# Three places instead of four for each of two rings of gathers, two more page buffers, and four compression items asked for early

## The chip, the cores and the metric

One NeuronCore of a Trainium2 chip runs the whole program. The metric is the time of one execution on the device, in us; shown is the median of three.

## The reference, cut to what matters

One layer of a decoder for 256 prompt tokens and 8 x 4 sample tokens, all in float32: an input projection; stick-breaking attention (part A) and native sparse attention (part B: compressed, selected and window keys) over a paged cache; an output projection; a layer norm; and a feed-forward part that picks single neurons out of a table of 16384.

```python
def nsa_cmp_slc(...):            # part B, sample tokens: 8 sequences, 16 cached pages each
    kcmp = compress(rows[0], ...)  # windows of 32 rows, stride 16, through w1, gelu, w2
    vcmp = compress(rows[1], ...)
    ...                            # scores on kcmp choose 16 blocks of 64; attend to them and to the window
def peer_ffn(x, w_query, sub_keys, u_tab, v_tab):
    q = (xc @ w_query).reshape(PEER_TBLOCK, PEER_HEADS, 2, PEER_QDIM // 2)
    s = jnp.einsum('thcd,ckd->thck', q, sub_keys)
    ...                            # top 16 x 16 per head, best 16 of their sums: experts, gate
    act = jax.nn.gelu(jnp.einsum('thkd,td->thk', u_tab[experts], xc))
    return jnp.einsum('thk,thkd->td', gate * act, v_tab[experts])
```

Per token 8 heads x 16 experts: 128 rows of 8 KB out of `peer_u` and as many out of `peer_v`.

## The kernel before, in words

Every engine has an instruction stream of its own, written out by hand; semaphores alone order them. What the change touches:

**Slots.** The 288 tokens are 9 groups of 32, and each group has 32 slots of 4 experts. A slot is one gather of 128 rows of 8 KB (1 MB) from `peer_u`, a dot of it with the tokens on DVE (`gather_dot`, L2716), and later one gather from `peer_v`, which PE multiplies with a diagonal of weights (`value_rows`, L1955). All engines go through the slots as "ticks" s = 0 to 287. POOL (L2865) issues at tick s first u(s), then v(s - 11) (LAG = 11). u(s) waits until dot s - 4 is done, v(s) until PE has used v(s - 4): four places each, `u_ring` = ring[4:8], `v_ring` = ring[0:4] (L623). POOL runs in order, so whatever waits holds the rest. The weights of a round of 8 slots are made after its last dot (`act_start`, `act_finish`). The last 8 value gathers (TAIL, L242) alternate between both rings, since the dots no longer need theirs.

**The ring before that.** The same 8 places of 1 MB hold w_in, the pages of part A, w_out (L714) and then the 16 blocks of w_query, loaded by SP (`load`, L691; the place of block k is WQ_AT, L277). Place 8 (`AT_T + 4096`) is a ninth, for blocks 7 and 12. PE multiplies the blocks in order (`query_rows`, L1618), which yields the scores that DVE picks experts from. v(0) to v(3) wait until the last query block of their place is used.

**Pages.** The cached rows of part B come as items of 8 pages of 128 KB (1 MB), each page with its own DMA and a page number that the issuing engine first reads into a register (L462). `Background` (L302) gives each of them one of four buffers of 1 MB, `later_rows` (L604). 32 compression items (16 for keys, 16 for values) use buffers 2 and 3 alone, since buffers 0 and 1 hold w1. After them come, per half of the batch, 8 items ks, 2 kw, 8 vs, 2 vw, then 16 blocks of w_out and 16 of w_query for the last tokens, all through four buffers. A buffer is asked for again when PE has used what was in it (`later_used`). SP asks for the even pages and ACT, at ticks fixed in the program (`odd_pages` L1029, `odd_rows` L1038, ODD_PAGES L215), for the odd ones; of the first two compression items SP asks for all 8. PE handles compression item n at ticks from 10 + 5n // 2 (`taps`, L1678), the attention of the halves from ticks 92 and 111, ahead of the value matmuls of the same tick.

**SP's order around the gathers' start** (L714 to L746): w_out, w1, w_query 7, 0 to 6, 8 to 15; then it waits for `saved` (DVE has moved what the buffers overwrite, L2344), for h_in 5 (second tile normalized, L2382) and until block 12 is used; then compression item 0 and on.

Of the kernel before, what the change touches and what calls it, by code (L numbers as in the profile page):

```python
# [145 lines left out]
RING = 8  # L146
# [4 lines left out]
SWAP_AT = {STEP[ms[-1]] + 2: n for n, ms in enumerate(ROPED)}  # L151
ROUND = 8
# [47 lines left out]

def odd_page_ticks():
# [40 lines left out]
TAIL = SLOTS_ALL - 8  # L242


def tail_buffer(s):

    return "uv"[s % 2 == 0], (s - TAIL) // 2 % 4, (s - TAIL) // 8

# [28 lines left out]
WQ_AT = (4, 5, 6, 0, 1, 2, 3, 8, 0, 1, 2, 3, 8, 0, 1, 2)  # L277


WQ_LAST = [max(k for k in range(16) if WQ_AT[k] == s) for s in range(4)]  # L280


class Stream(Items):


    def __init__(self):
        super().__init__(RING + 1)
# [14 lines left out]
class Background(Items):  # L302


    def __init__(self):
        super().__init__(4)
        for i in range(4 * NB):
            self.add(("cmp", i // 16, i % 16), 2 + i % 2, 8)
        self.last[0] = self.last[1] = self.n - 1
        k = 0  # L310
        for h in range(2):
            for name, count, dmas in (("ks", 8, 8), ("kw", 2, 1), ("vs", 8, 8), ("vw", 2, 1)):
                for i in range(count):
# [57 lines left out]
def hybrid_step(nc, dram, outs):  # L371
    stream, later_items = Stream(), Background()
    with ExitStack() as ctx:
# [45 lines left out]
        ring = [words(AT_RING + 2048 * s, 2048) for s in range(RING)] + [words(AT_T + 4096, 2048)]  # L419
# [26 lines left out]
        ring_full = [sem(f"ring_full{s}") for s in range(RING + 1)]  # L446
# [157 lines left out]
        later_rows = [words(AT_T + 2048 * k, 2048) for k in range(4)]  # L604
# [18 lines left out]
        u_ring, v_ring = ring[4:8], ring[0:4]  # L623
# [5 lines left out]
        u_full = [sem(f"u_full{k}") for k in range(4)]  # L629
        v_full = [sem(f"v_full{k}") for k in range(4)]  # L630
# [3 lines left out]
        later_full = [sem(f"later_full{k}") for k in range(4)]  # L634
# [43 lines left out]
        def _(sp):  # L678
# [57 lines left out]

            sp.wait_ge(saved, 1)
# [41 lines left out]
        def _(act):  # L779
# [412 lines left out]
        def _(pe):  # L1192
# [762 lines left out]
            def value_rows(s):  # L1955
# [36 lines left out]
        def _(dve):  # L1992
# [723 lines left out]
            def gather_dot(s):  # L2716
# [3 lines left out]
                dve.wait_ge(u_full[j % 4], 16 * (s // 4 + 1))  # L2720
                u = u_ring[j % 4].rearrange("p (a b) -> p a b", a=KT)
# [78 lines left out]
        def _(pool):  # L2800
# [130 lines left out]
```

## Time and profile before

| what | us |
|---|---|
| median of three timed runs | 2435.42 (2432.51 to 2435.45) |
| the profiled execution, its own time | 2443.28 |
| its span | 2441.4 |
| PE busy | 1761.5 (72%) |
| DVE busy | 1301.4 (53%) |
| POOL busy | 863.1 (35%) |
| DMA: 961.30 MB, mean over the span | 394 GB/s |
| gathers, POOL's queue: 626.31 MB | 62.3% of 16 engines' time |
| SP's and ACT's transfers: 300.39 and 32.65 MB by queue | 31.8% and 4.0% |

The span counts from the first to the last record on the core. The page (a printed summary of the profile) says "the share of 16 engines' span" for a DMA queue: the time its packets took, over 16 engines and the span; overlapping packets can bring a share over 1. PE is the matrix engine, DVE the vector engine, ACT the scalar engine, POOL and SP the two that mostly issue DMAs here; a "q" behind a name is its queue of issued DMAs. L and a number is the line.

### The profile page before, as it was taken

The page shows a single profiled execution, that of the slowest core. Times are in us where ns is not written, and L with a number is a line of the kernel's source. Part 1 is how long each engine was busy: PE and PEld are TensorE (multiplying, and loading weights), DVE is VectorE, ACT ScalarE, POOL GpSimd, SP SyncE. Part 2 cuts the span into 40 slices and gives each one's busy share as a digit, 9 for nine tenths or more (in the row PEclk, how much of TensorE's full clock was granted, in tenths as well). Part 3 has the DMA queues.
Part 4 walks back from the last instruction along what each step waited for, and adds up shares of the span by engine and source line. Part 5 has one row for each costly group of instructions (what it writes and reads, how often), then busy time and mean ns, then how long its engine had stood idle before and what let it go on. Part 6 is the DMA issues. An engine that isn't in the chain of part 4 may idle for free.

```text
span 2441.4 us, 30395 instructions
## 1 busy us (share of the span) xinstructions
PE 1761.5 (72%) x9939; PEld 977.9 (40%) x9939; DVE 1301.4 (53%) x2580; ACT 356.9 (15%) x837; POOL 863.1 (35%) x595
## 2 busy tenths in 40 slices
PE   8999999989998987778675656869633333346334
PEld 6777766643786765556412212217300000000000
DVE  0600112352876886666959562345788754555553
ACT  0001111330411111210201020012210001012111
POOL 0000000000133433444424242324465677677673
PEclk9999999999998988888887877978755555555556
DMA  9989999998699999999999999999999999999997
GB/s 386 374 344 360 371 384 371 368 374 363 274 396 407 384 407 409 406 407 406 409 385 399 386 365 398 420 421 421 419 421 421 421 422 421 421 421 422 421 421 320
DMA packets 213311, 961.30 MB, mean 394 GB/s; under 512 B 23841, under 2 KB 89378, under 8 KB 122754
## 3 DMA queue, kind: packets, MB, share of 16 engines
q0 software_dynamic: 84432, 626.31, 62.3%
q1 hardware_dynamic: 92914, 300.39, 31.8%
q10 hardware_dynamic: 35808, 32.65, 4.0%
q8 instruction: 80, 1.31, 0.2%
q14 instruction: 77, 0.63, 0.1%
HBM read 952.77 MB, written 14.88 MB: 396 GB/s over the span
## 4 chain that ended last, share of the span: by engine, by line
DMA 43%; PE 41%; issue 5%; DVE 4%; ACTq 4%; POOL 1%; SPq 1%; ACT 1%; POOLq 0%; DVEq 0%
DMA sb<-in_peer_v,sb 24%; PE bank L1208 14%; DMA sb<-in_nsa_t 12%; PE bank L1688 6%; PE bank L1971 4%; DMA sb<-in_peer_u,sb 3%; PE bank L1574 3%; PE bank L1279 2%; PE bank L1621 2%; ACTq L462 2%; PE bank L1307 2%; DMA sb<-in_nsa_v 2%; DVE sb L2722 2%; DMA sb<-in_w_out 1%; PE bank L1886 1%
## 5 line engine op out<-in xcount | busy, mean ns | idle before, releaser
L2722 DVE CUSTOM_DVE_ANT_0 sb<-sb 128x2048 f32<-128x2048 f32 x288 | 659.4, 2292 | 411.0 <-DMA sb<-in_peer_u,sb 403.3
L1971 PE MATMUL bank<-sb 128*32 128x512 f32 x2304 | 461.2, 852 | 473.1 <-DMA sb<-in_peer_v,sb 447.2
L2838 POOL DMA_INDIRECT sb<-in_peer_v,sb x288 | 505.5, 1755 | 561.8 <-PE bank L1971 504.0
L2838 POOL DMA_INDIRECT sb<-in_peer_u,sb x288 | 349.3, 1213 | 433.5 <-DVE sb L2722 241.7
L1971 PEld LDWEIGHTS bank<-sb 128*32 128x32 f32 x2304 | 60.6, 126 | 773.8 <-DMA sb<-in_peer_v,sb 700.8
L1208 PE MATMUL bank<-sb 128*128 128x288 f32 x1408 | 352.1, 410 | 7.5 <-DMA sb<-in_tokens_t 7.5
L1688 PE MATMUL bank<-sb 128*128 128x256 f32 x1024 | 281.7, 435 | 86.6 <-DMA sb<-in_nsa_t 70.6
L1208 PEld LDWEIGHTS bank<-sb 128*128 128x128 f32 x1408 | 266.5, 191 | 92.1 <-issue 13.9
L1688 PEld LDWEIGHTS bank<-sb 128*128 128x128 f32 x1024 | 250.2, 310 | 130.7 <-DMA sb<-in_nsa_t 85.1
L1165 ACT ACTIVATE sb<-sb 128x32 f32<-128x32 f32 x288 | 86.2, 315 | 669.3 <-PE bank L1971 306.3
L2822 POOL DMA_DIRECT2D out_a<-sb x1 | 0.5, 545 | 503.9 <-PE bank L1307 503.9
L1754 PE MATMUL bank<-sb 128*32 128x512 f32 x128 | 71.7, 753 | 41.2 <-DMA sb<-in_nsa_t 41.2
L1808 PE MATMUL bank<-sb 128*32 128x256 f32 x256 | 62.0, 423 | 35.1 <-DMA sb<-in_nsa_v 35.1
L786 ACT ACTIVATE sb<-bank 128x288 f32<-128x288 f32 x44 | 18.1, 410 | 410.1 <-PE bank L1208 410.1
L969 ACT ACTIVATE sb<-sb 32x2048 f32<-32x2048 f32 x36 | 68.6, 1907 | 51.8 <-PE bank L1777 29.5
L1574 PE MATMUL bank<-sb 128*32 128x512 f32 (+1 forms) x256 | 71.8, 600 | 0.1
L1621 PE MATMUL bank<-sb 128*128 128x160 f32 (+1 forms) x512 | 71.0, 297 | 0.7 <-issue 0.7
L1621 PEld LDWEIGHTS bank<-sb 128*128 128x128 f32 x512 | 67.7, 191 | 3.3 <-ACT sb L982 2.2
L1307 PE MATMUL bank<-sb 128*32 128x512 f32 x512 | 61.5, 602 | 5.6 <-DMA sb<-in_a_v 5.5
L1886 PE MATMUL bank<-sb 128*128 128x128 f32 x512 | 62.5, 284 | 3.5 <-DMA sb<-in_w_query 3.5
L1886 PEld LDWEIGHTS bank<-sb 128*128 128x128 f32 x512 | 60.2, 198 | 11.7 <-DMA sb<-in_w_query 7.6
L1847 PE MATMUL bank<-sb 128*32 128x512 f32 x512 | 60.7, 622 | 2.0 <-DMA sb<-in_w_out 1.9
(412 smaller groups left out, 1486.9 us busy)
## 6 DMA issues: line engine op xcount, KB each, us to landing
sb<-in_a_k SPq DMA_DIRECT2D x128, 512.0 KB, 7.3
sb<-in_a_v SPq DMA_DIRECT2D x128, 512.0 KB, 7.1
sb<-in_w_in SPq DMA_DIRECT2D x43, 1024.0 KB, 9.4
sb<-in_w_out SPq DMA_DIRECT2D x32, 1024.0 KB, 20.9
sb<-in_w_query SPq DMA_DIRECT2D x32, 1024.0 KB, 10.0
sb<-in_nsa_t SPq DMA_DIRECT2D x200, 128.0 KB
sb<-in_nsa_t ACTq DMA_DIRECT2D x184, 128.0 KB
sb<-in_nsa_v SPq DMA_DIRECT2D x64, 128.0 KB
```

The costliest lines, as they stand in the source:

```text
L969: act.activation(replica(g)[32 * q:32 * q + 32], src, ACT.Copy).then_inc(rep_in, 1)
L1165: act.activation(diag[j % 4], const["fold"], ACT.Copy, scale=w8[:, r % 2, j:j + 1]).then_inc(diag_in, 1)
L1208: mm = pe.matmul(bank[step % 2][:, 0:T], w[:, kt * P:(kt + 1) * P], x_t[:, kt, :], start=(kt == 0), stop=(kt == KT - 1))
L1307: mm = pe.matmul(bank[(0 if half else 6) + c][r, :], z_t[:, half, 2 * pp + j, r], rows[b4][:, 1024 * j + 512 * c:1024 * j + 512 * c + 512] ...
L1574: mm = pe.matmul(bank[3 * (n % 2) + tt][own, :], mix(4 * kq + kt)[:, P * tt:P * tt + rows], w[:, kt, :], start=(kq == 0 and kt < parts), s ...
L1621: mm = pe.matmul(bank[5 if m == 1 else 1 if m == 2 else m % 2][:, 0:count], w[:, P * kt:P * kt + P], h_t[:, kt, 0:count], start=(kt == 0), ...
L1688: mm = pe.matmul(bank[(7, 3)[n % 2]][:, 0:256], rows[:, :, l], w1_one[:, :, l, :], start=(l == 0), stop=(l == 15), skip_group_check=True)
L1754: mm = pe.matmul(bank[((5, 6), (7, 2))[ph][c]][32 * b4:32 * b4 + 32, :], q_pad[:, 4 * h + b4, g], rows[:, 4 * c:4 * c + 4, g, :], start=(g ...
L1886: mm = pe.matmul(bank[2 + m % 2][:, 0:ROWS_2], w[:, P * kt:P * kt + P], h_t2[:, kt, :], start=(kt == 0), stop=(kt == KT - 1))
L1971: mm = pe.matmul(bank[g % 2][32 * c:32 * c + 32, :], diag[j % 4], rows[:, 512 * c:512 * c + 512], start=(s in FIRST), stop=(s in LAST), sk ...
L2722: dve.tensor_tensor_reduce(out=u, in0=u, in1=replica(g), scale=1.0, scalar=0.0, op0=ALU.mult, op1=ALU.add, accum_out=act8[:, r % 2, j:j + ...
L2838: pool.indirect_dma_start(rows[j % 4], None, dram[table], bass.IndirectOffsetOnAxis(ap=idx, axis=0)).then_inc(full[j % 4], 16)
```

## The change: what it does

- `PLACES = 3`: u_ring is ring[4:7], v_ring ring[0:3]; u(s) waits for dot s - 3, v(s) for PE's use of v(s - 3).
- v(0), v(1), v(2) are issued at ticks 9, 10, 11 instead of 11, 12, 13; v(3) and on at tick s + 11 as before.
- TAIL is the last 6 slots, alternating between the rings, each place once.
- `later_rows` gets ring[7] and ring[3]: the compression items go through buffers 2 to 5, the rest through six. ACT asks for the odd pages of item n + 4, not n + 2, when item n is used, and for the first six ks items at ticks 82, 84, 87, 89, 90, 91 instead of 89 to 92 for the first four.
- The ninth place for query blocks is gone. Blocks 0 to 7 go to places 4, 5, 6, 7, 1, 2, 0, 3, blocks 8 to 15 to 1, 2, 0 in turn.
- SP asks for all 8 pages of compression items 0 to 3 itself, and earlier: item 0 after `saved`, ahead of the query blocks; item 1 after h_in 5; item 2 when block 3 is used (its place 7 is buffer 4); item 3 when block 7 is used (place 3, buffer 5). Item 4 and on come behind block 15, even pages by SP.

```diff
+PLACES = 3
...
+FIRST_ODD = (82, 84, 87, 89, 90, 91)
...
-            at = order[k - 4][3] + 1 if k >= 4 else NSA_AT[0] - 3 + k
+            at = order[k - 6][3] + 1 if k >= 6 else FIRST_ODD[k]
...
-TAIL = SLOTS_ALL - 8
+TAIL = SLOTS_ALL - 2 * PLACES
...
-    return "uv"[s % 2 == 0], (s - TAIL) // 2 % 4, (s - TAIL) // 8
+    return "uv"[s % 2 == 0], (s - TAIL) // 2
...
-WQ_AT = (4, 5, 6, 0, 1, 2, 3, 8, 0, 1, 2, 3, 8, 0, 1, 2)
+WQ_AT = (4, 5, 6, 7, 1, 2, 0, 3, 1, 2, 0, 1, 2, 0, 1, 2)
...
-        super().__init__(4)
+        super().__init__(6)
         for i in range(4 * NB):
-            self.add(("cmp", i // 16, i % 16), 2 + i % 2, 8)
+            self.add(("cmp", i // 16, i % 16), 2 + i % 4, 8)
         self.last[0] = self.last[1] = self.n - 1
-        k = 0
+        k = 2
...
-                    self.add((name, h, i), k % 4, dmas)
+                    self.add((name, h, i), k % 6, dmas)
...
-        later_rows = [words(AT_T + 2048 * k, 2048) for k in range(4)]
+        later_rows = [words(AT_T + 2048 * k, 2048) for k in range(4)] + [ring[7], ring[3]]
...
-        u_ring, v_ring = ring[4:8], ring[0:4]
+        u_ring, v_ring = ring[4:4 + PLACES], ring[0:PLACES]
...
-            for k in (7, *range(7), *range(8, 16)):
-                load(("wq", k), dram["w_query"][k].rearrange("p k n -> p (k n)"))
...
             sp.wait_ge(saved, 1)
+            cached_rows(0, 0, range(8))
+            query_blocks(range(8))
             sp.wait_ge(h_in, 5)
-            sp.wait_ge(item_used, stream.used["wq", 12])
+            cached_rows(0, 1, range(8))
+            sp.wait_ge(item_used, stream.used["wq", 3])
+            cached_rows(0, 2, range(8))
+            query_blocks(range(8, 11))
+            sp.wait_ge(item_used, stream.used["wq", 7])
+            cached_rows(0, 3, range(8))
+            query_blocks(range(11, 16))
             for kv in range(2):
                 for i in range(2 * NB):
-                    later_pages(("cmp", kv, i), 8 * i, lambda pg: dram["nsa_t"][bass.ds(pg, 1), kv],
-                                range(8) if kv == 0 and i < 2 else range(0, 8, 2))
+                    if kv or i >= 4:
+                        cached_rows(kv, i, range(0, 8, 2))
...
-                    if 2 * NB * kv + i + 2 < 4 * NB:
-                        odd_pages(2 * NB * kv + i + 2)
+                    if 2 * NB * kv + i + 4 < 4 * NB:
+                        odd_pages(2 * NB * kv + i + 4)
...
-                if s >= 4:
-                    hold(u_used, s - 3)
+                if s >= PLACES:
+                    hold(u_used, s - PLACES + 1)
...
-                    ring_of, k, turn = tail_buffer(s)
-                    if turn:
-                        hold(v_used, s - 7)
-                    elif ring_of == "v":
-                        hold(v_used, TAIL - 3 + k)
+                    ring_of, k = tail_buffer(s)
+                    if ring_of == "v":
+                        hold(v_used, TAIL - PLACES + 1 + k)
                     else:
-                        hold(u_used, SLOTS_ALL - 3 + k)
+                        hold(u_used, SLOTS_ALL - PLACES + 1 + k)
...
-                if s >= LAG:
+                if LAG - 2 <= s < LAG + PLACES - 2:
+                    v_of(s - LAG + 2)
+                elif s >= LAG + PLACES:
                     v_of(s - LAG)
```

`query_blocks(ks)` loads the named blocks of w_query as the removed loop did, and `cached_rows(kv, i, pages)` is the removed call of `later_pages`. Elsewhere the change only writes `s % PLACES` and `s // PLACES` for the place of a slot and its count.

## Rows read from the trace of the kernel before

**Rows 1.** The page, parts 4 and 5: the chain, and the dots

```profile
DMA 43%; PE 41%; issue 5%; DVE 4%; ACTq 4%; POOL 1%; SPq 1%; ACT 1%; POOLq 0%; DVEq 0%
...
L2722 DVE CUSTOM_DVE_ANT_0 sb<-sb 128x2048 f32<-128x2048 f32 x288 | 659.4, 2292 | 411.0 <-DMA sb<-in_peer_u,sb 403.3
```

**Rows 2.** Windows: us, each engine's busy us, PE clock, DMA share, GB/s

```profile
602.00:618.00 16.00, 16.00 (x53) 6.58 (x55) 2.39 (x7) 0.69 (x1) 0.00 (x0) 1.00 0.04 15
636.00:648.00 12.00, 11.52 (x172) 10.97 (x171) 10.56 (x44) 7.13 (x11) 0.17 (x1) 1.00 0.02 8
648.00:699.00 51.00, 51.00 (x361) 47.76 (x361) 47.95 (x130) 19.34 (x38) 11.40 (x12) 1.00 1.00 410
699.00:702.00 3.00, 3.00 (x23) 2.68 (x22) 2.73 (x9) 0.85 (x3) 1.88 (x2) 1.00 0.63 175
790.00:839.00 49.00, 43.43 (x221) 32.78 (x220) 41.90 (x95) 7.04 (x30) 12.87 (x14) 0.89 1.02 399
839.00:842.00 3.00, 3.00 (x15) 3.00 (x14) 2.79 (x9) 0.00 (x0) 2.60 (x2) 1.00 0.48 123
1240.00:1280.00 40.00, 29.97 (x127) 8.40 (x130) 13.74 (x30) 1.24 (x4) 9.89 (x8) 0.91 1.03 379
1433.00:1438.00 5.00, 5.00 (x53) 1.98 (x55) 1.57 (x3) 0.00 (x0) 0.09 (x1) 0.78 0.31 94
1524.00:2402.00 878.00, 455.11 (x2481) 128.34 (x2479) 514.73 (x905) 120.64 (x276) 520.71 (x318) 0.60 1.01 421
2402.00:2406.00 4.00, 1.93 (x8) 0.20 (x8) 2.94 (x9) 0.44 (x3) 2.54 (x1) 0.50 0.62 219
```

**Rows 3.** Timeline of SP's queue: start, us to the last one's end, count

```profile
589.34 0.43 SPq L693 DMA_DIRECT2D sb<-in_w_query  x1
...
617.15 6.33 SPq L693 DMA_DIRECT2D sb<-in_w_query  x7
...
647.52 36.97 SPq L693 DMA_DIRECT2D sb<-in_w_query  x8
...
699.01 13.70 SPq L731 DMA_DIRECT2D sb<-in_nsa_t  x16
```

**Rows 4.** Waits of SP, 560 to 1000: total us, times, longest

```profile
SPq L739 <- PE bank L1621: 9.9, 1, 9.9
```

**Rows 5.** Timeline of DVE: what fires `saved` and h_in 5

```profile
563.72 0.68 DVE L2344 COPY sb<-bank 32x512 f32<-32x512 f32 x1
...
632.72 2.34 DVE L2382 SCALAR_TENSOR_TENSOR sb<-sb 32x2048 f32<-32x2048 f32 x1
```

**Rows 6.** Timeline of PE: query block 11, item 0's taps, first value matmul

```profile
684.63 4.61 PE L1621 MATMUL bank<-sb 128*128 128x160 f32 x32
...
714.15 9.05 PE L1688 MATMUL bank<-sb 128*128 128x256 f32 x32 [3.20 <-issue]
...
723.13 1.07 PE L1971 MATMUL bank<-sb 128*32 128x512 f32 x8
```

**Rows 7.** Timeline of POOL: gathers, in brackets its idle time before

```profile
687.42 0.94 POOL L2838 DMA_INDIRECT sb<-in_peer_u,sb  x1 [3.12 <-DVE sb L2722]
...
699.72 0.94 POOL L2838 DMA_INDIRECT sb<-in_peer_v,sb  x1 [6.18 <-PE bank L1621]
...
725.04 2.46 POOL L2838 DMA_INDIRECT sb<-in_peer_v,sb  x1 [6.72 <-PE bank L1971]
...
1814.54 3.06 POOL L2838 DMA_INDIRECT sb<-in_peer_u,sb  x1 [5.90 <-DVE sb L2722]
...
2406.69 0.94 POOL L2838 DMA_INDIRECT sb<-in_peer_v,sb  x1 [2.15 <-PE bank L1971]
```

**Rows 8.** DMA issues, 640 to 700: count, KB each, median us to landing

```profile
sb<-in_w_query SPq DMA_DIRECT2D x8, 1024.0 KB, 10.0
```

**Rows 9.** The chain: a value gather from issue to landing, steady and last

```profile
1997.53 17.05 DMA sb<-in_peer_v,sb
...
2415.40 15.88 DMA sb<-in_peer_v,sb
```

More of the change, by code:

```diff
@@ L274, in add @@
         self.used[key] = self.n
-WQ_AT = (4, 5, 6, 0, 1, 2, 3, 8, 0, 1, 2, 3, 8, 0, 1, 2)
-WQ_LAST = [max(k for k in range(16) if WQ_AT[k] == s) for s in range(4)]
+WQ_AT = (4, 5, 6, 7, 1, 2, 0, 3, 1, 2, 0, 1, 2, 0, 1, 2)
+WQ_LAST = [max(k for k in range(16) if WQ_AT[k] == s) for s in range(PLACES)]
 class Stream(Items):
     def __init__(self):
-        super().__init__(RING + 1)
+        super().__init__(RING)
         order = []
@@ L318, in __init__ @@
             for i in range(16):
-                self.add((name, i), k % 4, 1)
+                self.add((name, i), k % 6, 1)
                 k += 1
@@ L418, in hybrid_step @@
         x_t = words(AT_X, KT, T)
-        ring = [words(AT_RING + 2048 * s, 2048) for s in range(RING)] + [words(AT_T + 4096, 2048)]
+        ring = [words(AT_RING + 2048 * s, 2048) for s in range(RING)]
         def mix(kt):
@@ L445, in hybrid_step @@
         item_used = sem("item_used")
-        ring_full = [sem(f"ring_full{s}") for s in range(RING + 1)]
+        ring_full = [sem(f"ring_full{s}") for s in range(RING)]
         consts_in, first_in, x_in, wg_in, rope_in, w1_in, pages_in = (sem(n) for n in (
@@ L628, in hybrid_step @@
         q_in, s_mm, s_in, gate_arg, gate_e, chosen = (sem(n) for n in ("q_in", "s_mm", "s_in", "gate_arg", "gate_e", "chosen"))
-        u_full = [sem(f"u_full{k}") for k in range(4)]
-        v_full = [sem(f"v_full{k}") for k in range(4)]
+        u_full = [sem(f"u_full{k}") for k in range(PLACES)]
+        v_full = [sem(f"v_full{k}") for k in range(PLACES)]
         u_used, v_used, act_arg, act_e, w_ready, diag_in, group_out, y_out = (sem(n) for n in (
@@ L633, in hybrid_step @@
         rep_in, rep_used = sem("rep_in"), sem("rep_used")
-        later_full = [sem(f"later_full{k}") for k in range(4)]
+        later_full = [sem(f"later_full{k}") for k in range(6)]
         later_used, w1_one_in, cmp_sum_out = sem("later_used"), sem("w1_one_in"), sem("cmp_sum_out")
@@ L1031, in odd_pages @@
                 rows, full = later_rows[later_items.slot["cmp", kv, i]], later_full[later_items.slot["cmp", kv, i]]
-                if n == 2:
+                if n == 4:
                     act.wait_ge(pages_in, 16)
@@ L1958, in value_rows @@
                     pe.wait_ge(group_out, 4 * (g - 1))
-                rows = v_ring[j % 4]
                 if s < TAIL:
-                    pe.wait_ge(v_full[j % 4], 16 * (s // 4 + 1))
+                    rows = v_ring[s % PLACES]
+                    pe.wait_ge(v_full[s % PLACES], 16 * (s // PLACES + 1))
                 else:
-                    ring_of, k, turn = tail_buffer(s)
+                    ring_of, k = tail_buffer(s)
                     rows = (v_ring if ring_of == "v" else u_ring)[k]
                     if ring_of == "v":
-                        pe.wait_ge(v_full[k], 16 * (TAIL // 4 + turn + 1))
+                        pe.wait_ge(v_full[k], 16 * (TAIL // PLACES + 1))
                     else:
-                        pe.wait_ge(u_full[k], 16 * (SLOTS_ALL // 4 + turn + 1))
+                        pe.wait_ge(u_full[k], 16 * (SLOTS_ALL // PLACES + 1))
                 pe.wait_ge(diag_in, s + 1)
@@ L2837, in gather @@
             def gather(table, rows, idx, full, j):
-                pool.indirect_dma_start(rows[j % 4], None, dram[table], bass.IndirectOffsetOnAxis(ap=idx, axis=0)).then_inc(full[j % 4], 16)
+                pool.indirect_dma_start(rows[j % PLACES], None, dram[table], bass.IndirectOffsetOnAxis(ap=idx, axis=0)).then_inc(full[j % PLACES], 16)
             def u_of(s):
@@ L2860, in v_of @@
                     return
-                if s >= 4:
-                    hold(v_used, s - 3)
+                if s >= PLACES:
+                    hold(v_used, s - PLACES + 1)
                 gather("peer_v", v_ring, expert[:, slot_group(s), slot_column(s):slot_column(s) + 1], v_full, s)
```

13 lines of the change are left out of this document (9 added, 4 removed).

## The prediction

> **What bounds the kernel now.** Read the chain of waits first: DMA holds 43% and PE 41% of it [rows 1]. Then the windows, whose last two columns are the busy share of the 16 DMA engines and their rate [rows 2]: the reader is to see that from 648 us to 2402 us the DMA engines are full, 1.00 to 1.03, but for gaps of a few us, and that before 648 us, while PE multiplies w_out and the first w_query blocks, they are nearly idle twice (602 to 618 at 0.04, 636 to 648 at 0.02). The change moves no byte more or fewer. So for most of the span the time is work plus idle of one server: it can fall only by work pulled ahead of 648 us and by gaps closed, and rise only by new gaps. My units: 1 MB in 8 KB rows costs 1.0486 / 0.421 = 2.49 us, a pages item of 1 MB in 1 KB rows 1.0486 / 0.379 = 2.77 us, the rate of 1240 to 1280, where little but pages moves [rows 2].
>
> **Part 1: items 0 and 1 ahead of the gathers.** SP today issues w_query 7 at 589.34 and seven more blocks from 617.15, and stands waiting after each lot [rows 3]; pages start at 699.01. The wait before them ended at 647.52 + 36.97 + 9.9 = 694.4 [rows 3, 4], so reading eight page numbers takes 4.6 us, and two items with their second reading took 13.7, so eight transfers take (13.7 - 4.6) / 2 = 4.55 us to issue. After the change:
> - Item 0 waits for `saved`, which fires at 564.4 [rows 5], so SP isn't held. Its eight transfers leave at about 594 to 598.5 and take the DMA time that w_query 7 had. Block 7 joins the lot at 617 to 624, which then runs 2.5 us longer, into the gap at 636. SP's next wait ends at 617.15 anyway, so the 9 us of issue cost nothing.
> - Item 1 waits for h_in 5, the offset of the normalization, which ends at 635.06 [rows 5]: reading to 639.7, issue to 644.2, landed by about 646, inside the gap [rows 2]. If that cover were gone, it would stand behind the first gathers and win nothing.
> Two items leave the full stretch: 2 x 2.77 = **-5.5 us** (bounds: -2.8 if item 1 misses the gap, -5.5).
>
> **Part 2: items 2 and 3 and three places for blocks 11 to 15.** SP's order is now item 2 (after block 3, 647.5), blocks 8 to 10, item 3 (after block 7, 668.9), blocks 11 to 15. Item 2 issues to about 656.6, so block 8 leaves at 656.6 and not at 647.5; PE wants it at 684.63 - 3 x 5.0 = 669.6 [rows 6], 13 us later (a block takes 5.0 us: block 11 starts at 684.63, and when 13 is used, v0 leaves, at 699.72 [rows 7]). Item 3 is read and issued from 668.9 to 678, so block 11 leaves at 678; PE wants it at 684.63 [rows 6], 6.6 us later, where these blocks land a median 10.0 us after issue today [rows 8]. But that 10.0 holds queueing that shrinks: one gather fewer is under way. Laid in the order of arrival from 649.5, the work up to block 11 (u0 to u6, items 2 and 3, blocks 8 to 11) is 11 x 2.49 + 2 x 2.77 = 32.9 us, which ends at 682.5. I take no stall of PE (bounds: 0 and 678 + 10.0 + 2.8 - 684.6 = 6.2 us); a gain is excluded, as PE has no wait in this stretch. Blocks 12 to 15 leave two block times (10.0 us) before use, against 10.0 [rows 8].
>
> **Part 3: POOL's order.** Value gather 0 now stands after u9 and not after u11. u9 leaves at 687.42, when today u10 does (both follow dot 6). v0 waits for block 13 and leaves at 699.72 [rows 7]; u10 and u11, which leave before it today, are queued behind it until 701 and 706, and DVE, which needs them for dots 10 and 11, waits with them; v1 and v2 wait for blocks 14 and 15. From 649.5 DMA has 18 transfers of 2.49 (u0 to u9, blocks 8 to 15) and two items: 50.4 us, so it runs dry at 699.9, and v0's data flows about 1.8 us after issue: 1.6 us of idle. Then v0 to v2 and u10 to u14 are 8 x 2.49 = 19.9 us, to 721.4. The next value gather needs place 0 back. PE's first value matmul starts at 723.13, behind item 0's taps (9.05 us from 714.15), neither of which the change moves [rows 6]. So v3 leaves at 725.04, when today v4 does [rows 7], and item 4 is asked for at about 723.5. Idle: 721.4 to about 725.1, 3.7 us. Today this stretch is fed by items 0 and 1 and has 3.0 x 0.37 = 1.1 us of idle [rows 2]. So **+4.2 us** (bounds 0 and 8: gathers held longer behind v0, or the tap items arriving sooner).
>
> **Part 4: deeper pages, shallower gathers, 730 to 1540.** The compression stage has 4 page buffers instead of 2 and the attention stage 6 instead of 4, with 6 gather places instead of 8: the number of megabytes that can be under way is the same. The gap at 839 to 842 (3 x 0.52 = 1.6 us) comes at the end of a stretch in which DVE is busy 41.9 of 49 us [rows 2]: buffers fill and wait for DVE. If PE gets its pages sooner at 730 to 790, DVE is ahead there and the gap goes: **-1.6 us** (bounds -1.6, +2). In the attention stage POOL and DVE stand behind PE, which waits for pages, and the engines idle 5 x 0.69 = 3.45 us at 1433 [rows 2]; pages two deeper shorten that. I take two thirds: **-2.3 us** (bounds -3.5, +3).
>
> **Part 5: three places where only gathers run.** At 1997.53 a value gather lands 17.05 us after issue [rows 9], in a cycle of 17.05 + 1.98 + 0.85 = 19.9 us for four places, 4.97 a slot. Three places make a cycle of 14.9 us and leave 14.9 - 2.8 = 12.1 us for landing. What an unloaded landing takes is bounded by the last eight gathers: the first is issued at 2406.69 [rows 7], the last lands at 2431.28 [rows 9], so the first landed by 2431.28 - 7 x 2.49 = 2413.9 at the latest, and 2.49 us of that is the one before it: 4.7 to 7.2 us. Twelve is well above it: the steady rate holds. What thins is the cover when DVE is away: 4.9 to 7.4 us instead of 9.9 to 12.4. The longest wait of POOL for a dot was 5.90 us, before 1814.54 [rows 7]. A dot there is 2.29 us [rows 1], and the dots behind the stall stand close together, so the gather is late by about one dot more: **+0.7 us** (bounds 0 and 10, two such waits times a slot).
>
> **Part 6: the end.** Only six of the last value gathers can be under way and not eight; 284 waits for value 280 and 286 for value 281. The last dot's data lands at T; value 276 + n can land at T + 2.49 (n + 1), the last, 287, at T + 29.9; a place is handed on 1.98 + 0.85 = 2.8 us after its landing. So with three places value 279 leaves at T + 2.5 + 2.8 = 5.3, 280 at 7.8, 281 at 10.3, 282 at 12.8, 284 at 15.3, 286 at 17.8. An unloaded landing of 4.7 us delays none of them by more than 0.1, one of 7.2 delays each by up to 2.6. **+0.9 us** (bounds 0, +2.6). The idle of 4 x 0.38 = 1.5 us at 2402 [rows 2] stays.
>
> **Sum.** -5.5 + 4.2 - 1.6 - 2.3 + 0.7 + 0.9 = -3.6 us. The profiled execution took 2443.28 us (span 2441.4), 7.9 us more than the median 2435.42 of the timed ones. 2443.28 - 3.6 = 2439.7; the same difference on the median gives **2431.8 us**. About 0.2%, 4.9 us, can be told from no change here.
>
> **Rivals.**
> A, the forecast: -3.6.
> B, all gaps close: v0's place costs no new idle (the early items let PE hand back value place 0 sooner, and today's 1.1 goes too), and attention's 3.45 goes wholly, with no loss at the end: -5.5 - 1.1 - 1.6 - 3.5 = -11.7, **2423.7**. For it: PE's taps wait for pages, not for arithmetic, in this part. Against: PE's 714.15 and 723.13 don't move.
> C, hidden anyway: DVE sets 790 to 839 [rows 2], its tick times don't move, so what was loaded early shows as a longer gap at 839. Parts 1 to 4 come to about 0, the rest +1.6: **2437.0**. For it: 41.9 of 49 us busy. Against: the megabytes are saved unless DVE is the bound on its own.
> D, slower by the query blocks: block 11 lands 6.2 us late as bounded above, block 14, issued when 11 is used, lands 12.8 us after issue and costs 2.1 more, everything behind block 15 (values, taps) moves by 6.2 + 2.1 = 8.3 us, and DMA, with three dot places, can't work ahead: -3.6 + 8.3 + 1.6 = +6.3, **2441.7**. It decides from a landing of 6.6 us for block 11 on. For it: the 10.0 [rows 8]. Against: the shorter queue.
> The Trainium skill speaks for D ("DMA: Bandwidth & Descriptors", Queues, rings and completion order): each DMA engine takes turns between the queue rows that have work, and SP's transfers share one ring on each engine. By that rule block 11 stands behind item 3 in SP's ring and gets every other turn; my sum goes by arrival instead. No row shows which holds when 1 KB and 8 KB rows mix.
> E, starved gathers: each time DVE is away longer than 4.9 us, a slot is lost; POOL's two longest waits for a dot behind 1750 cost 9.9 us: -3.6 + 9.9 = +6.3, **2441.7**. It decides if gathers issued after such a wait already land in the unloaded time. For it: 5.90 against a cover of 4.9 to 7.4. Against: two bounds at their worst ends.
>
> **How the numbers follow.** A 0.46 (its spread, some 3 us either way, lies 0.22 beyond -4.9 and 0.24 within), B 0.17 (faster), C 0.13 (0.10 same, 0.03 slower), D 0.13 (slower), E 0.11 (0.03 same, 0.08 slower). Faster 0.39, same 0.37, slower 0.24. A's own range is 2428 to 2436; to leave out no more than 2 in 10 the range reaches to B and a little past it, and to D and E and a little past: 2421.5 to 2443.5.
>
> **What would show it.** Part 1: page issues on SP at about 594 and 640, and a busy share well over 0.02 at 636 to 648. Part 2: PE without a wait for w_query before block 11; a wait there is D. Part 3: a gap of some 4 us at 721 to 725, v0 at about 699.7. Part 4: no gap at 839, and a smaller one than 3.45 us around 1433. Part 5: landings of 12 us in the steady stretch, a share of 1.01 there, and at most 1 us of idle near 1815. Part 6: last landing some 30.5 us behind the last dot's. The forecast is wrong if PE's first value matmul moves from 723 by more than 2 us, or if the full stretch behind 842 has new gaps of more than 3 us together.

## The result, and the profile after

The changed kernel is slower. Median of 15 runs 2444.35 us (2440.8 to 2446.21) against 2436.58 us (2432.51 to 2442.72) for the kernel before, measured beside it; ratio **1.0026**, 95% interval 1.0019 to 1.0033, that is +6.3 us (4.6 to 8.0). The forecast was 2431.8, -3.6 us. All differences in us below are ratio times 2436; a difference of two kernels' ratios is uncertain by some 3 us. Its profiled execution took 2446.21 us, span 2444.4.

The page, parts 4 and 5, against [rows 1]:

```profile
DMA 40%; PE 38%; DVE 10%; issue 6%; POOL 2%; ACTq 2%; SPq 1%; ACT 1%; POOLq 0%; DVEq 0%
...
L2738 DVE CUSTOM_DVE_ANT_0 sb<-sb 128x2048 f32<-128x2048 f32 x288 | 659.9, 2293 | 475.8 <-DMA sb<-in_peer_u,sb 471.3
```

The chain has moved from DMA and PE to DVE, 4% to 10%, and DVE's idle time before the dots grew from 411.0 to 475.8 us: dots wait more for their rows.

Windows, columns as in [rows 2], six of the old stretches and five new ones:

```profile
636.00:648.00 12.00, 11.51 (x173) 10.97 (x171) 10.67 (x45) 7.29 (x11) 0.00 (x0) 1.00 0.54 187
648.00:699.00 51.00, 46.79 (x315) 43.82 (x315) 47.61 (x131) 18.58 (x36) 9.45 (x10) 0.93 0.98 382
699.00:702.00 3.00, 3.00 (x23) 2.68 (x22) 2.77 (x10) 0.60 (x3) 0.00 (x0) 1.00 0.39 164
705.00:709.00 4.00, 4.00 (x30) 3.68 (x29) 2.73 (x6) 0.85 (x3) 2.23 (x2) 1.00 0.04 14
721.00:725.00 4.00, 4.00 (x19) 4.00 (x19) 2.30 (x2) 0.00 (x0) 0.50 (x1) 1.00 1.01 418
839.00:842.00 3.00, 3.00 (x18) 1.80 (x17) 1.76 (x6) 0.59 (x2) 0.71 (x2) 1.00 1.04 407
1433.00:1438.00 5.00, 1.93 (x8) 0.20 (x8) 3.09 (x8) 0.15 (x1) 0.93 (x1) 0.50 1.03 403
1524.00:2402.00 878.00, 445.29 (x2426) 122.91 (x2421) 515.51 (x905) 120.76 (x276) 523.40 (x317) 0.59 1.01 417
1810.00:1815.00 5.00, 1.94 (x8) 0.23 (x8) 4.83 (x11) 0.34 (x2) 4.39 (x3) 0.50 0.57 192
1811.00:1812.00 1.00, 0.00 (x0) 0.00 (x0) 0.93 (x7) 0.00 (x0) 0.86 (x1) 0.50 0.06 25
1815.00:1820.00 5.00, 0.00 (x0) 0.00 (x0) 3.70 (x9) 0.03 (x1) 4.09 (x4) 0.50 0.98 357
```

The reader is to see five things. The gap at 636 to 648 is half filled (0.02 to 0.54): item 1 went there. A new gap stands at 705 to 709 (0.04). At 721 to 725, where I forecast one, there is none (1.01). The gaps at 839 and at 1433 are gone. And the long stretch in which only gathers and blocks move, 1524 to 2402, runs at 417 GB/s where it ran at 421: 1% of 878 us, and 1810 to 1815 is a hole in it (0.57, at 1811 only 0.06), 1815 to 1820 its edge (357 GB/s).

SP's queue, against [rows 3]:

```profile
594.48 3.97 SPq L732 DMA_DIRECT2D sb<-in_nsa_t  x8
617.39 6.44 SPq L697 DMA_DIRECT2D sb<-in_w_query  x8
639.86 18.17 SPq L732 DMA_DIRECT2D sb<-in_nsa_t  x16
658.08 6.26 SPq L697 DMA_DIRECT2D sb<-in_w_query  x3
673.62 4.12 SPq L732 DMA_DIRECT2D sb<-in_nsa_t  x8
677.78 23.66 SPq L697 DMA_DIRECT2D sb<-in_w_query  x5
```

PE and POOL, against [rows 6] and [rows 7] (every line of the code stands 16 further down; in brackets the idle time before and what ended it):

```profile
689.15 6.84 PE L1637 MATMUL bank<-sb 128*128 128x160 f32 x32 [4.21 <-DMA sb<-in_w_query]
...
725.76 1.06 PE L1987 MATMUL bank<-sb 128*32 128x512 f32 x8
```

```profile
706.46 2.08 POOL L2854 DMA_INDIRECT sb<-in_peer_v,sb  x1 [17.79 <-PE bank L1637]
...
1808.80 3.05 POOL L2854 DMA_INDIRECT sb<-in_peer_u,sb  x1 [5.86 <-DVE sb L2738]
...
1870.90 2.21 POOL L2854 DMA_INDIRECT sb<-in_peer_u,sb  x1 [5.89 <-DVE sb L2738]
...
1931.18 3.05 POOL L2854 DMA_INDIRECT sb<-in_peer_u,sb  x1 [4.45 <-DVE sb L2738]
```

What DVE does before the first of these three: its dot of 1797.36 ends at 1799.6, then it picks experts for a later group until its next dot at 1805.69, and POOL waits for that dot.

```profile
1797.36 2.29 DVE L2738 CUSTOM_DVE_ANT_0 sb<-sb 128x2048 f32<-128x2048 f32 x1
...
1805.69 2.29 DVE L2738 CUSTOM_DVE_ANT_0 sb<-sb 128x2048 f32<-128x2048 f32 x1 [0.18 <-DVE sb L2488]
```

Three transfers of the chain of waits, from issue to landing: w_query block 11, a value gather of the steady stretch [rows 9], and one of the end, behind which the queue runs nearly empty for a moment (0.64 of its time busy from 2402 to 2406):

```profile
677.78 11.23 DMA sb<-in_w_query
...
1990.78 12.10 DMA sb<-in_peer_v,sb
...
2400.47 7.63 DMA sb<-in_peer_v,sb
```

To place the loss I added up the bytes of each trace's packets, and took the time at which each kernel had moved so many megabytes, less that of the kernel before (us):

| megabytes moved | at (before) | after | order | late4 | late_u | late_v | tail8 | both | vlate | three | one_early |
|---|---|---|---|---|---|---|---|---|---|---|---|
| 240 | 666 | -2.6 | -4.5 | -3.9 | -1.1 | -2.1 | -5.1 | -3.7 | -4.8 | +0.1 | -2.6 |
| 260 | 717 | +2.8 | -1.3 | +2.4 | +2.1 | +4.3 | +0.9 | -0.4 | -1.7 | +4.7 | -1.8 |
| 320 | 868 | -0.3 | -4.4 | -0.5 | -0.5 | +1.6 | -2.8 | -3.5 | -5.3 | +1.8 | -4.6 |
| 560 | 1471 | -5.6 | -9.4 | -4.9 | -6.0 | -3.3 | -8.5 | -7.9 | -10.4 | +0.6 | -4.5 |
| 700 | 1807 | -5.8 | -8.6 | -5.0 | -6.2 | -3.8 | -8.7 | -9.0 | -9.8 | +2.2 | -3.5 |
| 760 | 1949 | +0.8 | -3.6 | -5.0 | -5.3 | +2.0 | -2.6 | -8.9 | -9.8 | +7.9 | -3.3 |
| 960 | 2427 | +2.6 | -3.3 | -5.6 | -1.9 | -1.0 | -5.3 | -8.3 | -8.9 | +8.2 | -3.3 |

Column "after" tells where this pair of profiles differs: ahead by 2.6, back by 2.8 at 717, level at 868, 5.8 ahead at 1807, and 8.4 us lost from there to the end. The profiled execution of before was 7 us above its median, so the end of the table (+2.6, spans 2444.4 - 2441.4 = +3.0) is less than the timed +6.3.

### The profile page after: what moved, and what is told of

Read it like the earlier page. It is cut to its first block, busy times and chain, and to the rows that moved or that the text cites. A ratio compares the mean times of both kernels' runs of the same rounds, so it can differ in the third digit from the quotient of the medians.

```text
span 2444.4 us, 30396 instructions
## 1 busy us (share of the span) xinstructions
PE 1740.5 (71%) x9939; PEld 965.0 (39%) x9939; DVE 1300.6 (53%) x2580; ACT 357.9 (15%) x837; POOL 824.2 (34%) x595
## 3 DMA queue, kind: packets, MB, share of 16 engines
q8 instruction: 80, 1.31, 0.2%
## 4 chain that ended last, share of the span: by engine, by line
DMA 40%; PE 38%; DVE 10%; issue 6%; POOL 2%; ACTq 2%; SPq 1%; ACT 1%; POOLq 0%; DVEq 0%
DMA sb<-in_peer_v,sb 23%; PE bank L1224 14%; DMA sb<-in_peer_u,sb 11%; PE bank L1987 4%; DVE sb L2738 4%; PE bank L1704 3%; PE bank L1590 3%; POOL sb L2854 2%; PE bank L1637 2%; PE bank L1295 2%; DMA sb<-in_nsa_t 2%; PE bank L1323 2%; DMA sb<-in_nsa_v 2%; ACTq L1061 1%; PE bank L1902 1%
## 5 line engine op out<-in xcount | busy, mean ns | idle before, releaser
L2738 DVE CUSTOM_DVE_ANT_0 sb<-sb 128x2048 f32<-128x2048 f32 x288 | 659.9, 2293 | 475.8 <-DMA sb<-in_peer_u,sb 471.3
L2854 POOL DMA_INDIRECT sb<-in_peer_v,sb x288 | 492.8, 1711 | 472.8 <-PE bank L1987 391.4
L2854 POOL DMA_INDIRECT sb<-in_peer_u,sb x288 | 323.1, 1122 | 566.8 <-DVE sb L2738 369.1
L1224 PEld LDWEIGHTS bank<-sb 128*128 128x128 f32 x1408 | 265.8, 191 | 92.5 <-issue 13.9
L1704 PE MATMUL bank<-sb 128*128 128x256 f32 x1024 | 256.6, 406 | 7.6 <-issue 6.9
L1704 PEld LDWEIGHTS bank<-sb 128*128 128x128 f32 x1024 | 237.8, 307 | 38.6 <-issue 33.2
L1637 PEld LDWEIGHTS bank<-sb 128*128 128x128 f32 x512 | 70.0, 195 | 7.6 <-issue 5.8
L1902 PEld LDWEIGHTS bank<-sb 128*128 128x128 f32 x512 | 58.4, 193 | 7.5 <-issue 7.5
```

The source lines that it names most:

```text
L1224: mm = pe.matmul(bank[step % 2][:, 0:T], w[:, kt * P:(kt + 1) * P], x_t[:, kt, :], start=(kt == 0), stop=(kt == KT - 1))
L1637: mm = pe.matmul(bank[5 if m == 1 else 1 if m == 2 else m % 2][:, 0:count], w[:, P * kt:P * kt + P], h_t[:, kt, 0:count], start=(kt == 0), ...
L1704: mm = pe.matmul(bank[(7, 3)[n % 2]][:, 0:256], rows[:, :, l], w1_one[:, :, l, :], start=(l == 0), stop=(l == 15), skip_group_check=True)
L1902: mm = pe.matmul(bank[2 + m % 2][:, 0:ROWS_2], w[:, P * kt:P * kt + P], h_t2[:, kt, :], start=(kt == 0), stop=(kt == KT - 1))
L2738: dve.tensor_tensor_reduce(out=u, in0=u, in1=replica(g), scale=1.0, scalar=0.0, op0=ALU.mult, op1=ALU.add, accum_out=act8[:, r % 2, j:j + ...
L2854: pool.indirect_dma_start(rows[j % PLACES], None, dram[table], bass.IndirectOffsetOnAxis(ap=idx, axis=0)).then_inc(full[j % PLACES], 16)
```

## The experiments

Twelve runs follow: the nine further kernels of the table, shallow, and vlate and the kernel before once more (vlate_again, before_again).

**Four places again at the end (late4).** The places change from slot 164 on, when no page is loaded any more; `place_free(s)` is the slot 3 back, from `WIDE_AT` on 4 back, and PE and DVE read the same `PLACE`:

```diff
-TAIL = SLOTS_ALL - 2 * PLACES
+WIDE_AT = 164
+TAIL = SLOTS_ALL - 8
+PLACE = [s % PLACES for s in range(WIDE_AT)] + [PLACES]
+while len(PLACE) < SLOTS_ALL:
+    PLACE.append(PLACE[-4])
...
+                if s == WIDE_AT:
+                    pool.wait_ge(later_used, later_items.n)
+                elif s >= PLACES:
+                    hold(u_used, place_free(s))
```

> The changed kernel, but from slot 164 on (issued at about 1765 us, when the last w_query block has left page buffers 4 and 5) the gathers take four places a kind again, and eight for the last eight values. Theory S (starved gathers): in the trace of the changed kernel the same megabytes are 5.8 us ahead of before at 1800 us and 0.8 us behind at 1950, with POOL waits of 5.86 and 5.89 us before 1808.80 and 1870.90, and about 1.9 us more are lost after 2300. With four places there the run is 6.6 + 1.5 = about 8 us faster than the changed kernel: ratio to before about 0.999 (median 2434 to 2438). Rival Q (the late w_query block 11 and what follows it sets the loss) and rival R (the loss is in the order of transfers in the attention stage): no change against the changed kernel, ratio 1.0026.

Measured: 0.9995 (0.9986 to 1.0004), median 2437.07: 7.6 us faster than the changed kernel. **Three places alone (three)** is the reverse, the kernel before with `PLACES = 3` in the rings, their waits and the tail, and nothing put into the two free places:

> The kernel before with three places a kind for the gathers and nothing else: page buffers, compression items, order of SP and POOL as before, the two places given up stay empty. Theory S: 6.6 + 1.9 = 8.5 us slower than before, perhaps more in the attention stage where no deeper pages make up for it: ratio 1.0035 or more. Rival Q: 0, ratio 1.000. Rival R (order of transfers): 0 to +2 us.

Measured: 1.0071 (1.0057 to 1.0084), 2454.59, +17 us. Theory S, slower with three places, stands in both; its size in the second was twice my 8.5, so about half of that loss is not explained by it. In that kernel only ten buffers are filled where before and the changed kernel fill twelve, and it is 4.7 us behind at 717 already; how the rest is spread its profile can't tell, since that execution (2449.83) was the fastest of its five. What before has in 1800 to 1950 us, and in the window with the hole:

```profile
1800.00:1950.00 150.00, 57.42 (x244) 6.10 (x240) 126.96 (x298) 9.64 (x35) 90.08 (x60) 0.50 1.01 421
1810.00:1815.00 5.00, 1.96 (x12) 0.20 (x8) 4.49 (x14) 0.50 (x3) 0.46 (x1) 0.50 1.02 426
```

The changed kernel:

```profile
1800.00:1950.00 150.00, 56.10 (x232) 5.88 (x232) 121.41 (x287) 9.95 (x36) 91.05 (x60) 0.50 0.99 403
```

late4:

```profile
1800.00:1950.00 150.00, 56.63 (x240) 6.09 (x240) 124.52 (x293) 9.95 (x36) 91.03 (x61) 0.50 1.01 421
1810.00:1815.00 5.00, 1.93 (x8) 0.23 (x8) 4.83 (x11) 0.36 (x2) 4.39 (x3) 0.50 1.02 423
```

```profile
1809.35 3.05 POOL L2864 DMA_INDIRECT sb<-in_peer_u,sb  x1 [2.56 <-DVE sb L2748]
```

421 against 403 GB/s over 150 us is 2.7 MB, 6.4 us: the hole of 1810 and its edge are its first part (some 3.5 us), and the rest lies behind the POOL waits of 1870 and 1931 shown above.

What makes the hole is not the length of POOL's wait. Counted from the first, it is dot gather 172 that waits 5.86 us in the changed kernel, and 173 that waits 2.56 us in late4, behind the same dot (169). The kernel before waits 5.90 us at its dot gather 173 too [rows 7], and its window has no hole (1.02); late4 itself waits 5.90 us at 1868.63, and its share stays at 1. With four places POOL has issued one dot gather and one value gather more before it stops, and these keep the DMA engines busy through the wait. The hole comes late in it: POOL is let go at 1808.80, that gather's issue alone takes 3.05 us, and the share falls to 0.75 at 1809, 0.35 at 1810 and 0.06 at 1811. Behind 1870.90 and 1931.18 it is smaller, 246 GB/s at 1874 and 213 at 1935.

**Which of the two rings (late_u, late_v).** late4, with the wait of a three-place ring put back in one of the rings from slot 164 on:

```diff
 # late_u, in v_of
-                if s >= PLACES and s != WIDE_AT:
-                    hold(v_used, place_free(s))
+                if s >= PLACES:
+                    hold(v_used, s - PLACES + 1)
 # late_v, in u_of
-                elif s >= PLACES:
-                    hold(u_used, place_free(s))
+                if s >= PLACES:
+                    hold(u_used, s - PLACES + 1)
```

> As late4, but from slot 164 on a value gather still waits for the value three slots back, as with three places; dots have four. Theory U (it is the dots' places that count: while DVE is away POOL stands at the u gather and the values behind it stand with it, so a fourth dot place alone moves the point at which POOL stops by a whole slot of 4.97 us): as late4, ratio 0.9995, no dip at 1810 us. Rival M (gathers interleave one to one, so the scarcer kind sets how many are under way): as the changed kernel, 1.0026. Rival T (only the total under way counts): half way, 1.001.

> As late4, but from slot 164 on a dot gather still waits for the dot three slots back, and values have four places. Theory U: as the changed kernel in the stretch 1800 to 1950, ratio 1.0020 (the last eight values have their eight places, which gives 1.5 back). Rival M: 1.0026. Rival T: half way, 1.001.

late_u: 1.0015 (1.0006 to 1.0024). Its trace:

```profile
1800.00:1950.00 150.00, 56.34 (x236) 6.10 (x240) 124.20 (x291) 9.95 (x36) 98.53 (x60) 0.50 1.01 419
1810.00:1815.00 5.00, 1.94 (x8) 0.23 (x8) 4.83 (x11) 0.34 (x2) 4.39 (x3) 0.50 1.01 421
```

```profile
1809.07 3.05 POOL L2864 DMA_INDIRECT sb<-in_peer_u,sb  x1 [2.56 <-DVE sb L2748]
...
2295.51 2.91 POOL L2864 DMA_INDIRECT sb<-in_peer_v,sb  x1 [4.58 <-PE bank L1997]
```

late_v: 1.0018 (1.0009 to 1.0027). Its trace:

```profile
1800.00:1950.00 150.00, 56.43 (x236) 5.90 (x232) 123.43 (x291) 9.63 (x35) 80.91 (x60) 0.50 0.99 405
1810.00:1815.00 5.00, 1.97 (x12) 0.23 (x8) 4.69 (x17) 1.07 (x4) 3.82 (x2) 0.50 0.57 202
```

```profile
1810.87 3.05 POOL L2864 DMA_INDIRECT sb<-in_peer_u,sb  x1 [5.90 <-DVE sb L2748]
```

At 1810 theory U holds: with four dot places and three for values the hole is not there (1.01), with three dot places and four for values it is as in the changed kernel (0.57, POOL's wait 5.90). But the whole of late_u's time did not come back: in the table it loses 3.4 us behind 1949, where late4 loses none, and the second row above shows a value gather held 4.58 us before 2295 us. By the times alone T (half way) fits both as well. So: near 1810 it is the dots' places; for the whole stretch up to the end the value places count too, and late_u's 1.0015 is not the 0.9995 of theory U.

**The end alone (tail8).** late4 with `WIDE_AT = 264`.

> As late4, but the fourth places are taken from slot 264 on, so that 1750 to 2300 us run with three and only the end with four a kind and eight for the last eight values. It splits late4's 7.6 us: by the traces 1.9 us of the changed kernel's loss lie behind 2350 us and 6.6 at 1800 to 1950, so 1.9 faster than the changed kernel, ratio 1.0018. If the tail were the main term (my Part 6 bound 2.6): at most 1.0015.

Measured: 1.0011 (1.0001 to 1.0021), 3.7 us faster than the changed kernel, twice the 1.9 expected and beyond my bound of 2.6, though 1.9 is inside the interval. In the table tail8 loses 6.1 us from 1807 to 1949, as the changed kernel does (6.6), and gains 2.7 behind it, where the changed kernel loses 1.8. But order and three, whose end is that of the changed kernel, lose only 0.3 there, so what the end costs stays between 0.3 and some 4 us.

**Items 2 and 3 behind the query blocks (order).**

```diff
-            sp.wait_ge(item_used, stream.used["wq", 3])
-            cached_rows(0, 2, range(8))
-            query_blocks(range(8, 11))
-            sp.wait_ge(item_used, stream.used["wq", 7])
-            cached_rows(0, 3, range(8))
-            query_blocks(range(11, 16))
+            query_blocks(range(8, 16))
+            cached_rows(0, 2, range(8))
+            cached_rows(0, 3, range(8))
```

> The changed kernel, but SP asks for compression items 2 and 3 only behind w_query block 15, so that blocks 8 to 15 are not held behind them. Rival Q: PE has no wait of 4.2 us at 685 us, value gather 0 leaves at 700 and not at 706.5, and the 4 us reach the end: 2440, ratio 1.001. Theory H (hidden): PE's wait goes and the gap at 700 to 709 us shrinks, but DVE, busy 44 of 49 us at 790 to 839, takes it back: 320 MB are moved by 867 us as in both kernels, and the time stays at the changed kernel's within 1.5 us, ratio 1.0026.

Measured: 1.0015 (1.0006 to 1.0024), 2441.24, 2.7 us faster than the changed kernel, about as much as can be told apart. PE in its trace, and the window of the new gap:

```profile
683.53 4.61 PE L1634 MATMUL bank<-sb 128*128 128x160 f32 x32
...
717.92 1.06 PE L1984 MATMUL bank<-sb 128*32 128x512 f32 x8
```

```profile
705.00:709.00 4.00, 4.00 (x31) 3.72 (x29) 2.08 (x6) 0.30 (x1) 2.43 (x2) 1.00 1.04 411
```

PE's wait of 4.2 us is gone, its first value matmul is at 717.92 and not at 725.76, the gap at 705 is closed. In the table the lead of 4.1 us lasts, through the DVE stretch, to 560 MB, so in this trace DVE doesn't take it back, against H; the time lies between Q's 1.001 and H's 1.0026, nearer to Q's.

**One item early, four places kept (one_early).** The kernel before; item 0 in page buffer 3 (`3 - i % 2` for `2 + i % 2`, so all compression items change buffers), asked for behind h_in 5 and ahead of w_query block 8:

```diff
-            for k in (7, *range(7), *range(8, 16)):
+            for k in (7, *range(7)):
...
             sp.wait_ge(h_in, 5)
+            later_pages(("cmp", 0, 0), 0, lambda pg: dram["nsa_t"][bass.ds(pg, 1), 0])
+            for k in range(8, 16):
+                load(("wq", k), dram["w_query"][k].rearrange("p k n -> p (k n)"))
             sp.wait_ge(item_used, stream.used["wq", 12])
```

> The kernel before with item 0 of the compression pages asked for in the idle gap at 636 to 648 us (behind h_in 5), and nothing else changed (four places, page buffers as before). My prediction's Part 1: 1 MB leaves the full stretch, -2.8 us, ratio 0.9989. Theory H: the megabyte is ahead at 700 us and not at 867 us, since DVE sets the time between 790 and 840: 0, ratio 1.000; the gap at 839 to 842 us grows from 1.6 to some 4 us.

Measured: 0.9988 (0.9979 to 0.9998), 2434.89, -2.9 us (-5.1 to -0.5): what Part 1 of the prediction says of one item, and H's 0 lies just outside the interval. In the table its 4.6 us at 868 hold the gap of 839 as well.

**Both corrections (both), and two variants of it.** shallow: `2 + k % 4` for `k % 6` in the attention stage and behind it, with ACT's ticks to match. vlate: `if s >= LAG: v_of(s - LAG)` for the two branches.

> The changed kernel with both corrections together: items 2 and 3 asked for behind w_query block 15, and four places a kind again from slot 164 on. If the terms add: order was 0.0011 below the changed kernel, late4 0.0031 below it, so 1.0026 - 0.0042 = 0.9984, median 2434. By the traces the order's 4.2 us last to the end; then it is 4 us below late4: 0.9978. If one takes the other's place (the query-block stall covers a gather wait later): 0.9995 as late4.

> As the run both, but the attention stage and the second layer's blocks use four page buffers (2 to 5) in place of six; the compression stage keeps four. Theory P (the trace of before against the changed one: 5.6 us gained between 1320 and 1480 us by the deeper pages): 5.6 us slower than both, or more, since the gathers have three places there and ten megabytes are in flight instead of twelve. Rival V (the profiled execution of before had an untypical gap at 1433; it took 7 us more than the median): within 1.5 us of both.

> As the run both, but value gathers 0 to 2 follow u gathers 11 to 13 again, as in the kernel before, and not u gathers 9 to 11. My Part 3: 3 to 4 us of the new idle at 700 to 725 us go, ratio some 0.0013 below both. Theory H (DVE takes it back between 790 and 839): same as both within 1 us.

both: 0.9996 (0.9987 to 1.0005); the terms did not add in the times, though in the table it is 3.9 us ahead of late4 at 1949 and 2.7 at the end. Whether the order's part is smaller in most executions stays open: the intervals of both and late4 overlap widely. shallow: 0.9998 (0.9989 to 1.0007): theory P's 5.6 us are excluded, the two deeper page buffers of the attention stage bring nothing that can be told. vlate: **0.9987** (0.9978 to 0.9996), below the kernel before and the changed one. It is 2.2 us below the run both by the ratios, 0.9 by the medians (2434.19 and 2435.06), and their two profiled spans are 2432.4 and 2432.1: no difference between these two is shown. Repeated:

> The run vlate once more (items 2 and 3 behind w_query block 15, values 0 to 2 behind u gathers 11 to 13, four places a kind from slot 164 on), beside late_u and late_v on one chip: 0.9987 again, if that was no luck of the chip; the bound below which it counts as faster than before is 0.998.

0.9990 (0.9981 to 0.9999), median 2434.95: both intervals exclude no change, but the bound of 0.998 is missed: 2.4 to 3.2 us, less than the 0.2% that the prediction took as the least that can be told from no change.

**A second profile of the kernel before (before_again).**

> The kernel before once more, for a second profile. Theory V: no gap of 3.45 us at 1433 us, and 560 MB moved about 4 us earlier than in the first profile (1466 instead of 1470.6). Theory P: the same gap.

It took 2442.65 us:

```profile
716.00:776.00 60.00, 50.32 (x249) 38.96 (x247) 33.04 (x68) 5.96 (x25) 25.94 (x20) 0.90 0.95 372
839.00:842.00 3.00, 3.00 (x19) 2.50 (x12) 2.90 (x6) 0.21 (x1) 2.21 (x1) 1.00 1.02 399
1320.00:1380.00 60.00, 41.51 (x234) 19.88 (x238) 34.73 (x87) 2.35 (x10) 17.37 (x14) 0.80 0.95 364
1433.00:1438.00 5.00, 4.65 (x44) 1.83 (x40) 4.76 (x7) 0.72 (x1) 3.01 (x2) 1.00 1.03 379
```

The gap of 1433 is not there (1.03), nor that of 839; in their place 716 to 776 and 1320 to 1380 have a share of 0.95, some 4.7 us idle each by their packets. The same windows of both, then of shallow:

```profile
1320.00:1380.00 60.00, 45.47 (x253) 20.87 (x254) 35.49 (x83) 1.74 (x6) 17.29 (x13) 0.84 1.03 390
1433.00:1438.00 5.00, 1.02 (x8) 0.23 (x8) 2.30 (x2) 2.12 (x2) 0.00 (x0) 0.50 1.03 404
```

```profile
1320.00:1380.00 60.00, 40.80 (x233) 18.79 (x232) 38.77 (x99) 2.38 (x8) 14.99 (x13) 0.89 1.04 397
1433.00:1438.00 5.00, 1.37 (x8) 0.20 (x8) 1.33 (x5) 3.97 (x4) 2.55 (x2) 0.50 1.02 401
```

Neither has such a gap, with six page buffers or with four. V's first half holds, its second (560 MB at 1466) does not: the idle time lies elsewhere in each execution, while their spans are alike (2441.4 and 2440.9). Both profiled executions of this kernel took some 6 us more than its median, so every column of the table above is measured from a slow base.

## Why the prediction was wrong

Both mechanisms that made the kernel slower stood in the prediction, as rivals, E (0.11) and D (0.13); they came true together, and neither was in the sum. The larger part is E's.

- **Part 1**, -5.5 for two items: right for the one item that was tested alone, -2.9 (2.8 forecast, interval -5.1 to -0.5); two alone weren't run. The unit of 2.77 us was misread, though: from 1240 to 1280 not little but pages moved, gathers were 6.41 of 15.18 MB, so an item in 1 KB rows costs more, by these numbers some 2.95 us (an estimate).
- **Part 2**, no stall of PE taken, bounds 0 and 6.2: **this step failed.** Block 11 left at 677.78, as worked out (678), and landed after 11.23 us, at 689.01; PE waited 4.21 us, v0 left at 706.46 and not at 699.7. My sum let work be done in order of arrival, which had it landed at 682.5, 6.5 us sooner. The packets of the two queues, q0 the gathers, q1 SP's, 675 to 681 us and then 684 to 690 us:

```profile
q0 software_dynamic: 238, 1.70, 70.1%
q1 hardware_dynamic: 708, 0.65, 32.2%
```

```profile
q0 software_dynamic: 176, 1.31, 52.5%
q1 hardware_dynamic: 170, 1.21, 48.4%
```

The first window is the end of item 3's 1 KB rows, behind which block 11 stood in SP's queue: 0.65 MB of them moved against 1.70 MB of gathers, all older than block 11. In the second both queues had 8 KB rows, and 1.21 MB moved against 1.31 MB of gathers, now of younger ones. Counted in 8 KB packets, by 689.01 dot gather 7, issued at 679.64, had moved all but one of its 128 rows (2.5 us), and block 12, which stands behind block 11, 87 of its 128 (1.7 us): together 4.2 of the 6.5 us. The Trainium skill's rule that I set against my sum ("DMA: Bandwidth & Descriptors", Queues, rings and completion order), turns between queues and one ring for all that SP issues, agrees with the second window, where the packets went nearly one for one (170 and 176). In the first they went three to one (708 and 238), so there a turn was not one packet of the profile. I had cited the rule and not let it into the sum.

The wait cost more than its own length. PE's granted clock fell while it waited, and the first four us and more of the block went by at 0.50, the lower of the two levels (1.2 GHz):

```profile
685.00:689.00 4.00, 0.00 (x0) 0.00 (x0) 3.86 (x9) 0.52 (x2) 0.93 (x1) 0.74 1.01 422
689.00:693.00 4.00, 3.85 (x14) 3.88 (x15) 3.66 (x9) 0.00 (x0) 0.00 (x0) 0.50 1.02 426
```

Block 11 took 6.84 us against 4.61 [rows 6], so v0 is 6.7 us late: 4.5 for block 11's start and 2.2 for the clock. late4, late_u, late_v and tail8 show the same wait (3.5 to 4.9 us) and a slow block behind it (6.1 to 7.0 us). Removed (order), the whole gave 2.7 us by the times, 4.1 in the trace.
- **Part 3**, +4.2 for v0's place in POOL's order: too large. No gap came at 721, and what vlate gives back against both (0.9 to 2.2 us) is within the noise. The step that failed is the one by which the change moves neither item 0's taps nor PE's first value matmul. In order, without the wait for block 11, the taps start at 710.52 and take 7.47 us (714.15 and 9.05 before), the first value matmul is at 717.92 and not at 723.13, and place 0 is handed back before the gap can open.
- **Part 4**, -1.6 and -2.3: not shown, and the compression stage's four buffers were never taken back alone. Both rested on gaps of one execution, which the second profile has elsewhere; shallow against both puts the deeper pages at 0.2 us. A gap of the trace was taken for a property of the kernel.
- **Part 5**, +0.7: **this step failed, in size and in kind.** The steady landing is right to the digit (12.1 forecast, 12.10 above). But I priced one wait of POOL, and only as one gather late by one dot; the 0.7 has no working on record. There are three such waits, before 1808.80, 1870.90 and 1931.18. They are no longer than with four places (5.86, 5.89 and 4.45 us, against 5.90, 5.90 and 4.45 in the kernel before), and behind each the DMA engines run short. An estimate of the cover is the steady landing less the landing with little under way: 12.10 - 7.63 = 4.5 us with three places, 17.05 - 7.63 = 9.4 with four, where I had 4.9 to 7.4. It puts the first two waits beyond the cover of three places and all within that of four, but not the third, 4.45 us, behind which 1935 still has only 213 GB/s: it is a rough measure. What follows is not one late gather but a queue that empties and fills again (192, then 357 GB/s), 6.4 us in all by the rows of 1800 to 1950, and late4 got it back. That was rival E, whose price was its two waits (9.9 us).
- **Part 6**, +0.9, bound 2.6: its size is not settled. The landing at 2400.47 took 7.63 us, above my bound of 7.2. From the start of the last dot to that of the last value matmul it is 29.9 us in the kernel before, 29.8 in tail8, 34.0 in the changed kernel and 32.5 in order and three, where the prediction looked for some 30.5 to the last landing. But by megabytes moved the loss against before is 1.8 us in the changed kernel and 0.3 in the other two, and tail8's times say 3.7.

With what the runs give: -5.5 (two items, one of them tested) + 2.7 (blocks) + 0.9 to 2.2 (v order, not shown) + 0 (attention) + 7.6 (places in the gathers' stretch, the end with it) = 5.7 to 7.0, against +6.3 measured. Of these only the 7.6 stands clear of the noise, and the terms did not add in the run both. And vlate, which keeps items 0 and 1 early and has neither the wait for block 11, nor the early v0, nor three places behind slot 164, gained 2.4 to 3.2 us and not 5.5: 2 to 3 us stay open. It is chance that +6.3 is what the prediction gave for D alone and for E alone: D's blocks cost 2.7 us and not 8.3, E's waits with the end 7.6 and not 9.9 (and E's sum kept the 0.7 that the 9.9 replaces).

## What to carry to other kernels

When a buffer is taken from a prefetching ring, don't price the steady state (it holds as long as the landing fits): find the longest absence of the engine that gives places back, see whether the transfers that its places hold last through it and through the issue of the next one, and if they don't, charge the refill of the queue, at each such absence. A stage that no longer uses the buffers it was given should hand them back. And take a second profile before a gap of a few us goes into a sum.

## What was not expected

Two executions of one program, with spans of 2441.4 and 2440.9 us, have their idle time in other places: 3.45 us at 1433 in one, 4.7 at 1320 to 1380 in the other. And behind the empty queue of 1811 the gathers of 1 MB took some 9 us to come back to the steady rate (192 GB/s at 1810 to 1815, 357 at 1815 to 1820, against 421), longer than the 7.63 us in which one landed with little under way; why is not shown.
